# A fused two-block network kernel: the square root of each norm read straight from the sum's PSUM bank, and constant products in TensorE's gaps

## The reference, cut to what matters

```python
def rms_norm(x, g):
    xf = x.astype(jnp.float32)
    y = xf * lax.rsqrt(jnp.mean(xf * xf, axis=-1, keepdims=True) + EPS)
    return (y * g.astype(jnp.float32)).astype(x.dtype)
...
def _head_group_norm(o):
    mu = jnp.mean(o, -1, keepdims=True)
    var = jnp.mean(jnp.square(o - mu), -1, keepdims=True)
    return (o - mu) * lax.rsqrt(var + LN_EPS)
```

## Time and profile before

| | |
|---|---|
| median of three runs | 2226.35 us (2225.97 to 2227.18) |
| profiled execution, its own time | 2227.84 us |
| profiled execution, span of its instructions | 2226.1 us |
| mean granted TensorE clock | 0.983 |
| busy: PE, DVE, ACT | 2089.9, 947.8, 565.6 us |
| DMA | 621.20 MB, mean 279 GB/s |

### The profile page before, as it was taken

How to read it: one execution, slowest core, us unless ns; L and a number is a source line. 1 busy time by engine, 2 the same in 40 slices (tenths; PEclk the granted TensorE clock), 3 DMA queues, 4 the chain that set the end, 5 groups by cost and what they waited for, 6 DMA issues and landing times.

```text
span 2226.1 us, 30636 instructions
## 1 busy us (share of the span) xinstructions
PE 2089.9 (94%) x12726; PEld 1446.1 (65%) x12726; DVE 947.8 (43%) x1872; ACT 565.6 (25%) x1056; POOL 0.8 (0%) x6
## 2 busy tenths in 40 slices
PE   7999999999999999999988899999987799999986
PEld 6867779998877789998976444443334444443333
DVE  7899735552743345566365411211113521211112
ACT  2124123331135033344345311111112311111112
POOL 0000000000000000000000000000000000000000
PEclk9999999999999999999999999999999999999999
DMA  6435664446435654433240999999999599999995
GB/s 269 154 152 227 249 243 152 186 175 260 170 117 214 251 205 181 188 122 154 78 188 28 409 420 427 426 425 428 424 426 427 197 422 424 427 425 428 426 426 212
DMA packets 50077, 621.20 MB, mean 279 GB/s; under 512 B 5552, under 2 KB 5680, under 8 KB 12080
## 3 DMA queue, kind: packets, MB, share of 16 engines
q1 hardware_dynamic: 49824, 619.53, 67.9%
q10 hardware_dynamic: 144, 0.13, 0.0%
HBM read 618.59 MB, written 1.05 MB: 278 GB/s over the span
## 4 chain that ended last, share of the span: by engine, by line
PE 73%; DMA 15%; DVE 9%; ACT 2%; issue 1%; SPq 0%; ACTq 0%; DVEq 0%
PE bank L650 19%; DMA ring<-in_experts 12%; PE bank L1315 12%; PE bank L1338 7%; DVE wide L1983 3%; PE bank L863 3%; PE bank L864 3%; PE bank L865 3%; DMA arena<-in_experts 3%; PE sums L865 3%; PE sums L864 3%; PE sums L863 3%; PE sums L1348 2%; PE bank L1006 2%; PE bank L1008 2%; PE bank L1007 2%
## 5 line engine op out<-in xcount | busy, mean ns | idle before, releaser
L650 PE MATMUL bank<-h,ring 128*128 128x256 f32 x1568 | 347.1, 382 | 0.0
L650 PEld LDWEIGHTS bank<-h,ring 128*128 128x128 f32 x1568 | 298.1, 191 | 48.3 <-issue 6.5
L2220 DVE TENSOR_TENSOR ring_split<-ring,arena_split 128x2048 fp32r<-128x2048 f32 x64 | 144.1, 2288 | 149.5 <-ACT arena_split L1604 149.5
L2676 DVE TENSOR_TENSOR wide<-bank,wide 128x256 f32<-128x256 f32 x64 | 27.2, 425 | 386.7 <-ACT wide L1801 386.7
L2683 DVE SCALAR_TENSOR_TENSOR scratch_split<-bank,small,wide_split 128x512 fp32r<-128x512 f32 x64 | 48.0, 750 | 272.4 <-ACT wide_split L1809 272.4
L1604 ACT ACTIVATE arena_split<-ring 128x2048 fp32r<-128x2048 f32 x64 | 119.3, 1906 | 156.6 <-PE sums L865 144.1
L1315 PE MATMUL bank<-ring,h 128*64 128x512 f32 x640 | 143.6, 595 | 15.2 <-DMA ring<-in_experts 15.2
L863 PE MATMUL bank<-h_split,arena_split 128*128 128x256 f32 x512 | 147.6, 288 | 7.1 <-DVE scratch_split L2243 7.1
L864 PE MATMUL bank<-scratch_split,arena_split 128*128 128x256 f32 x512 | 146.7, 287 | 0.0
L865 PE MATMUL bank<-h_split,ring_split 128*128 128x256 f32 x512 | 146.6, 286 | 0.0
L1315 PE MATMUL bank<-arena,wide 128*64 128x512 f32 x608 | 137.0, 595 | 9.8 <-DMA arena<-in_experts 9.7
(11 more groups left out here) (382 smaller groups left out, 3544.1 us busy)
## 6 DMA issues: line engine op xcount, KB each, us to landing
ring<-in_stream SPq DMA_DIRECT2D x99, 2048.0 KB, 7.6
ring<-in_experts SPq DMA_DIRECT2D x96, 2048.0 KB, 29.1
arena<-in_experts SPq DMA_DIRECT2D x72, 2048.0 KB, 26.9
arena<-in_experts SPq DMA_DIRECT2D x22, 1024.0 KB, 23.9
stat<-in_experts SPq DMA_DIRECT2D x22, 512.0 KB, 24.7
scratch<-in_experts SPq DMA_DIRECT2D x22, 512.0 KB, 26.5
extra<-in_experts SPq DMA_DIRECT2D x2, 2048.0 KB, 26.1
arena<-in_stream SPq DMA_DIRECT2D x1, 2048.0 KB, 29.1
```

The costliest lines, as they stand in the source:

```text
L650: mm = pe.matmul(dst, a, b, start=(first and i == 0), stop=(i == len(terms) - 1))
L2220: dve.tensor_tensor(split["ring"][:, slot, 2048 * part:2048 * part + 2048], v, HI[("up", "down")[part]][:, j % 2, :].bitcast(F32), ALU.sub ...
```

## The change

Two things are done at once.

**The root.** `variance` goes, and so do the written-out forms for the latents and the heads: 11 + 4 + 2 instructions of VectorE. `root` now waits for the sum itself, reads the PSUM bank and computes sqrt(sum/n + eps) in one activation, with 1/n as an immediate scale and epsilon as a bias. The bias is a column of 128x1 in `small`, which two memsets at the start of VectorE's queue fill. The latents' root becomes two activations, since their scales differ.

**Products of constants.** `keep_clock(n)` puts n products on TensorE's queue, each the identity by 256 columns of the constants, fp32, into half a bank that nobody reads. They wait for nothing. Their places: 8 behind the sum of `("mix", 0)`; 6 ahead of pair 3's scores in layer 0; in both layers 3 ahead of the wait for the convolution branch and 7 ahead of the MLP; at each of the four layer norms 3 between the two sums, and 10 behind the second one except at the last; in each `moe` 7 ahead of the ranking, 2 behind it and 3 ahead of the last `spread`; 4 in the pooling mixer. That makes 104 products.

```diff
+            def keep_clock(n, dump=sums[2]):
+                for _ in range(n):
+                    pe.matmul(dump[:, T:2 * T], ident, con[:, 0:T], start=True, stop=True, skip_group_check=True)
...
                 rms_sum(("mix", l))
+                if l == 0:
+                    keep_clock(8)
...
                 for pair in range(HEADS + 2):
+                    if l == 0 and pair == HEADS // 2 - 1:
+                        keep_clock(6)
...
+                keep_clock(3)
                 S.wait(pe, "y_ready", "conv", l)
...
                 mod_site(l, MOD_MLP[1])
+                keep_clock(7)
...
                 filled(mm, "sum", "post", i, s)
+                keep_clock(3)
...
                 filled(mm, "sum2", "post", i, s)
+                if (i, s) != (1, 1):
+                    keep_clock(10)
...
                 rows(1, 1)
+                keep_clock(7)
...
+                keep_clock(2, sums[1])
                 zero_sums("read", "rank", i)
...
+                keep_clock(3, banks[3])
                 pe.wait_ge(S.sem(f"moe{i}_y_kept"), rounds * EXPERTS + 1)
...
             pool_rows(3)
+            keep_clock(4)
             pool_band_of(2)
...
-            def root(tag, n=T):
-                S.wait(act, "variance", *tag)
-                S.give(act.activation(stat[:, 1, 0:n], stat[:, 0, 0:n], ACT.Sqrt), "root", *tag)
+            def root(tag, n, eps, fill):
+                bank = take(act, *fill)
+                ins = act.activation(stat[:, 1, 0:T], bank[:, 0:T], ACT.Sqrt, scale=1.0 / n, bias=eps)
+                read("root", S.give(ins, "root", *tag), *fill)
...
-            def variance(tag, n, eps, fill, col=0):
-                bank = take(dve, *fill)
-                ins = dve.tensor_scalar(stat[:, 0, 0:T], bank[:, 0:T], 1.0 / n, eps, ALU.mult, ALU.add)
-                read("variance", S.give(ins, "variance", *tag), *fill)
...
             dve.wait_ge(S.sem("tokens_landed"), 16)
+            dve.memset(eps_rms, EPS)
+            S.give(dve.memset(eps_ln, LN_EPS), "dve_setup", "eps_ready")
             S.give(dve.memset(small[:, 256:384], 0.0), "dve_setup", "zero_ready")
```

More of the change, by code:

```diff
@@ L451, in two_blocks_kernel @@
         loggam = small[:, 0:8]
+        eps_rms, eps_ln = small[:, 116:117], small[:, 117:118]
         def norm_col(i, s, which, k):
@@ L1434, in done, with latent_root @@
                 read("act_read", S.give(ins, "act_read"), *fill)
-            def root(tag, n=T):
-                S.wait(act, "variance", *tag)
-                S.give(act.activation(stat[:, 1, 0:n], stat[:, 0, 0:n], ACT.Sqrt), "root", *tag)
+            def root(tag, n, eps, fill):
+                bank = take(act, *fill)
+                ins = act.activation(stat[:, 1, 0:T], bank[:, 0:T], ACT.Sqrt, scale=1.0 / n, bias=eps)
+                read("root", S.give(ins, "root", *tag), *fill)
+            def latent_root(l):
+                bank = take(act, "sum", "latent", l)
+                act.activation(stat[:, 1, 0:T], bank[:, 0:T], ACT.Sqrt, scale=1.0 / QR, bias=eps_rms)
+                ins = act.activation(stat[:, 1, T:2 * T], bank[:, T:2 * T], ACT.Sqrt, scale=1.0 / KVR, bias=eps_rms)
+                read("root", S.give(ins, "root", "latent", l), "sum", "latent", l)
             def copy_out(dst, src, kind, key, fill, scale=None):
@@ L1534, in block_1 @@
                         square_x(pair, "mix", 0)
-                root(("mix", l))
+                if l == 0:
+                    S.wait(act, "dve_setup", "eps_ready")
+                root(("mix", l), D, eps_rms, ("sum", "mix", l))
                 if l == 0:
@@ L1557, in block_1 @@
                     gate_inputs(l)
-                root(("latent", l), 512)
+                latent_root(l)
                 tanh_gates(l, 10)
@@ L1631, in block_1 @@
                     square_x(pair, "mlp", l)
-                root(("mlp", l))
+                root(("mlp", l), D, eps_rms, ("sum", "mlp", l))
                 for i in range(4):
@@ L1693, in _ @@
             squares_after(LAYERS - 1, "mlp", "final")
-            root(("final",))
+            root(("final",), D, eps_rms, ("sum2", "final"))
             S.wait(act, "chunk_used", max(m for m in range(C_AB) if slot_of(m) == VALUE_SLOT))
@@ L1740, in _ @@
             for i in range(2):
-                S.wait(act, "variance", "head", i)
-                S.give(act.activation(smax[:, 2 + i, :], smax[:, 2 + i, :], ACT.Sqrt), "root", "head", i)
+                bank = take(act, "sum2", "head", i)
+                ins = act.activation(smax[:, 2 + i, :], bank[:, :], ACT.Sqrt, scale=1.0 / P, bias=eps_ln)
+                read("root", S.give(ins, "root", "head", i), "sum2", "head", i)
             keep("nv")
@@ L2168, in block_1 @@
                     rotate(take(dve, "in", l, 5), A["kp"], "key_rotated", ("in", l, 5), l)
-                bank = take(dve, "sum", "latent", l)
-                dve.tensor_scalar(stat[:, 0, 0:T], bank[:, 0:T], 1.0 / QR, EPS, ALU.mult, ALU.add)
-                ins = dve.tensor_scalar(stat[:, 0, T:2 * T], bank[:, T:2 * T], 1.0 / KVR, EPS, ALU.mult, ALU.add)
-                read("variance", S.give(ins, "variance", "latent", l), "sum", "latent", l)
                 inverse_root(("latent", l), 512)
@@ L2235, in block_1 @@
                 tag = ("mlp", l)
-                variance(tag, D, EPS, ("sum", *tag))
                 inverse_root(tag)
@@ L2400, in _ @@
             for i in range(2):
-                bank = take(dve, "sum2", "head", i)
-                ins = dve.tensor_scalar(smax[:, 2 + i, :], bank[:, :], 1.0 / P, LN_EPS, ALU.mult, ALU.add)
-                read("variance", S.give(ins, "variance", "head", i), "sum2", "head", i)
-            for i in range(2):
                 S.wait(dve, "root", "head", i)
```

8 lines of the change are left out of this document (2 added, 6 removed).

## The result

The changed kernel takes 2211.73 us (median of 4 runs, 2209.77 to 2213.11) against 2226.16 for the kernel before in the same set: a ratio of 0.9929, 95% interval 0.9914 to 0.9944 (estimated from the single runs, so not quite the quotient of the two medians). A second set gave 2211.48 (5 runs) against 2228.47, 0.9925 (0.9911 to 0.9939). It is faster by 14 to 17 us. The forecast of 2206.0 was 5.7 us too low; the range of 2201 to 2217 held the time.

What follows compares the result with a forecast made beforehand. Four limits were said to take turns: VectorE and TensorE handing over, TensorE itself, the norm chains, and the experts' weight stream. Terms summed to 20.3 us, giving 2206.0 against the median of 2226.35; range 2201 to 2217.

Steps and rivals of the forecast that it cites:

- The root: At each norm, a 470 ns activation straight from PSUM saves 0.41 us; eight sites that count give 3.3 us.
- The first norm: Mix 0 at the kernel's start: the root saves 0.41 us and the memsets cost 0.05.
- Pair 3: Layer 0's attention: six products keep TensorE at full clock and VectorE can take it all, 3.4 us.
- The latent root: Layer 0: ScalarE takes both roots early, freeing 1.4 us of VectorE, of which 1.0 us counts.
- Clock at the first norm, MLPs, pooling: Filled waits keep full clock: 2.74 us at mix 0, 1.3 and 0.8 at the MLPs, 2.8 at pooling.
- The second experts: Second layer's layer norm and routing: 0.4 us root, 0.8 router, 1.9 gather, 3.1 us together.
- The first experts' cap: First layer's weight stream lacks releases only between 1240 and 1268, so 2.4 of TensorE's 3.3 us count.
- Rival B: Clock falls among narrow products and transposes despite fillers at pair 3 and routing; gain 14.1 us, 2212.2 us; chance 0.20.
- the 1.9 us: Routing: full clock shortens gather and zeroing by some 3 us, but VectorE's first copy limits the gain to 1.9.
- C: Whole kernel: clock falls as before and only the roots count, 4.7 us, 2221.7 us; chance 0.08.
- D: All filler sites: products run at half clock and overrun their waits by 37 us, 2258 us; chance 0.03.
- E: Three half-clock stretches between 1154 and 1182 move or vanish, up to 4 us more, 2202 us; chance 0.08.

Runs made afterwards that it cites:

- three things: Changed kernel with the memset wait between ScalarE's first two squares, 4 products ahead of pair 4's scores and more in the neighbourhood attention; 2209.80 us, ratio 0.9913.
- roots only: Changed kernel without any of its products of constants, so only the new roots; 2222.39 us, ratio 0.9979 to the kernel before.
- the overrun: Changed kernel with 20 instead of 10 products behind the sums of three of the four layer norms; 2224.06 us, ratio 0.9974.
- three and more: The kernel of three things with more products in the routing and 4 ahead of layer 0's last transposes; 2209.06 us, ratio 0.9908.
- early wait: Changed kernel with ScalarE's memset wait moved ahead of its first squares and the memsets to the start of VectorE's list; 2209.12 us, ratio 0.9921.

## Why the forecast was right, and where not

**The root** was right: 473 ns for 470, 0.40 to 0.41 us a norm. That the total came within 6 us owes a little to errors of opposite sign: the stretch of the first experts came out 0.84 us above its forecast and the one up to the first layer norm 0.33. That they stand against the miss is luck.

**The first norm** failed. The step "One norm costs 0.46 us ... The first goes" took the activation's start as given once its source was there, and priced the extra wait for the memsets at their 0.05 us. The wait took the table load out of its cover: 1.28 us on the path. Shown by the run with three things (15.26 us for the root instead of 16.62, behind a sum of the same length).

**Pair 3** failed, and is the larger part. The step was "VectorE, which waits 4.28 us for PE at 183.34, can take it all", 3.4 us. What that wait ends on are scores which themselves wait for a bank that ScalarE frees after VectorE's softmax; the idle time is real but the path to it goes through VectorE's own work before. Measured: the clock gave 3.2, VectorE let 1.4 of it through, and in the changed kernel's traces the clock then fell in the new wait, so the six products gave nothing (4.42 with, 4.62 without). Where it holds at pair 4 they give about 1.4.

**The latent root**, 1.0 us, was too small. TensorE's record at 112.31 comes without its wait in both kernels that have the new root, here roots only:

```profile
111.08 2.13 PE L651 MATMUL bank<-ring,arena 128*128 128x512 f32 x4
```

From just ahead of it to the next records TensorE's lead over before grows by 1.4 us (0.04 to 1.47 us in roots only, 1.64 to 3.07 in the changed kernel), all of what VectorE gained, where the forecast capped it by the wait of 1.02. The 1.50 us of roots only up to the convolution norm are 0.6 at the first norm, where a shorter part ran at half clock, 1.4 here, 0.4 of the convolution's root, less 0.9 that its longer stretch at pair 3 costs.

**Clock at the first norm, MLPs, pooling:** 2.74, 1.3 and 0.8, and 2.7 for 2.8 (3.12 less the root's 0.41). All products ended within the wait, as costed. How long such a stretch is varies (the first MLP's 3.4 us in roots only for 6.8 before), so these gains hold against this trace of before, and against another they could be some 1 us off, an estimate from these two.

**The second experts** gave 2.40 of 3.1 in this trace and 2.90 in the changed kernel's second one, so most of that gap is scatter.

**The first experts' cap** of 2.4 us was too tight. The stage gained 3.24, about TensorE's whole 3.3, and the overrun, where the stage loses at least what TensorE is late, shows the same with the other sign: the shortfall of the earlier trace rows between 1240 and 1268 understates what an earlier TensorE gives.

**Rival B** came out half true. At pair 3 the clock held, with transposes and narrow products around it. In the routing it held in the changed kernel's two traces and fell, with the same instructions, in others: the 1.9 us are there in five traces of eight. The forecast took a filled wait for a held clock; it should have taken the remaining 0.66 and 0.82 us as chances. The rule that the forecast cited with B, from the Trainium skill, "TensorE: Matmul & The Clock Gate", Part 4, that transposes do not count as busy, decides nothing here: with the waits of 0.66 and 0.82 filled (three and more, one trace) the clock held in both routings with their transposes where they were, and it had held in other traces with these waits open. C is out (2222.39 is its own time, within 0.7 us of its 2221.7), and so is D; its size was tried by the overrun, which gave nearly the products' own length. E did not come: the stretches between 1147 and 1175 stayed.

## What to carry to other kernels

Before idle time is counted as room for a gain, follow what ends it back until a different engine's work is reached: a wait of 4.28 us for scores could give way by 1.4 only, since behind it, by two steps, stood VectorE's own work. When a wait is added ahead of an activation that changes the function table, look where the load lands; a second wait just ahead of it put 1.28 us on the path here, and moving the wait one instruction up took them off. Products of constants in TensorE's gaps are worth having where the gap is long and cheap where they end in time, but too many hold the engine up (ten more behind a norm made the experts start 3.3 us later, six more in the routing 0.6), and a gap that is only nearly closed left the clock to chance, so such a kernel needs more than one trace.

## What was not expected of the hardware

- The first sum's 16 records took 5.10 to 6.51 us over the traces with nothing but the start of the kernel ahead of them, and the profile gives PEclk 1.00 in every window there. In each trace the first of them come every 0.43 us, as at half clock, and the last every 0.22, as at full; what varies is how many are slow (6 to 13). So the records' own durations, and not the granted clock, tell their speed at the start. The gain or loss is still there whole at the convolution norm: up to 1.4 us from one kernel's trace to another's, 0.3 us between two traces of the same kernel.
- In the first routing the clock fell behind a wait of 0.82 us in two of eight traces with the same instructions there, and held in six. The scatter of the kernel before follows its mean clock: over 41 runs in three sets, 2222.9 us on average at 0.986 (2 runs), 2228.1 at 0.983 (18), 2229.3 at 0.982 (12).
- A load of ScalarE's function table came ahead of a single wait (314.24, the root's wait ended at 317.24), but behind the second of two (15.32 in the changed kernel, 7.71 with the early wait).
